# A conditioning projection with the raw fp32 weights as the stationary operand, and grouped softmax in two attentions

## The reference, cut to what matters

```python
# window attention, per head (width 64), keys of this block of 128 and the one before
sc = einsum('qd,kd->qk', q, k) * 64 ** -0.5            # masked
m = maximum(max(sc), sink); e = exp(sc - m)
o = (e / (sum(e) + exp(sink - m))) @ v
# latent attention, per head (96 score dimensions, 64 value dimensions), causal
o = softmax(einsum('qd,kd->qk', q, k) * 96 ** -0.5) @ v
# conditioning, for each of the second block's two layers
mod  = silu(c)     @ w_ada[layer] + b_ada[layer]       # [1024] @ [1024, 6144]
modc = silu(c_ctx) @ w_ada[layer] + b_ada[layer]
```

## Time and profile before

| | |
|---|---|
| median of 3 runs (lowest, highest) | 4760.0 us (4756.5, 4763.3) |
| the profiled execution, its time | 4758.1 us |
| its span, first to last instruction | 4756.3 us |
| mean granted TensorE clock | 0.862 |
| PE, PEld, DVE, ACT busy | 3654.1, 2957.5, 2821.0, 2143.9 us |
| DMA, mean over the span | 135 GB/s |

### The profile page before, as it was taken

The page is one execution under the profiler, slowest core; times in us unless marked ns, Lnnn a source line. Parts: engine busy times, 40 slices in busy tenths (PEclk is TensorE's granted clock), DMA queues, the critical chain, the costliest instruction groups (busy, mean ns, idle before and its releaser), DMA issues. The chain is left out here.

```text
span 4756.3 us, 53669 instructions
## 1 busy us (share of the span) xinstructions
PE 3654.1 (77%) x17794; PEld 2957.5 (62%) x17794; DVE 2821.0 (59%) x3774; ACT 2143.9 (45%) x2746; POOL 647.1 (14%) x256
## 2 busy tenths in 40 slices
PE   6975999836866999666975567699897957656987
PEld 5654777635755777445965356588776846345865
DVE  4654999955746999776444544444344555444545
ACT  3433999823526999644433202233232434113433
POOL 0003433400004344300000230000000000310000
PEclk9576999977877999888998777899998978768998
DMA  2014999921017999775211001111121220011222
GB/s 91 1 45 179 419 418 416 402 74 38 1 64 308 417 417 417 298 255 186 60 38 24 1 1 45 37 62 62 58 62 37 73 43 1 1 38 65 97 78 81
DMA packets 158177, 643.31 MB, mean 135 GB/s; under 512 B 43482, under 2 KB 55228, under 8 KB 94396
## 3 DMA queue, kind: packets, MB, share of 16 engines
q1 hardware_dynamic: 135116, 617.42, 34.4%
q0 software_dynamic: 10592, 16.81, 1.0%
q10 hardware_dynamic: 12312, 7.10, 0.7%
HBM read 636.82 MB, written 24.35 MB: 139 GB/s over the span
## 5 line engine op out<-in xcount | busy, mean ns | idle before, releaser
L1413 DVE TENSOR_TENSOR w_low<-w_raw,w_high 128x2048 fp32r<-128x2048 f32 x392 | 881.9, 2283 | 61.6 <-ACT w_high L1477 59.8
L1477 ACT CAST w_high<-w_raw 128x2048 fp32r<-128x2048 f32 x392 | 746.3, 1911 | 78.3 <-DMA w_raw<-in_moe_down_dram 39.2
L485 PE MATMUL banks<-w_high,x_high 128*128 128x512 f32 (+3 forms) x1324 | 518.7, 392 | 145.9 <-DVE w_low L437 134.1
L485 PE MATMUL banks<-w_low,x_high 128*128 128x512 f32 (+3 forms) x1324 | 505.3, 382 | 0.0
L404 ACT CAST w_high<-w_raw 128x512 fp32r<-128x512 f32 (+3 forms) x321 | 190.7, 594 | 695.2 <-PE banks L485 621.1
L485 PE MATMUL banks<-w_high,x_low 128*128 128x512 f32 (+3 forms) x1324 | 503.9, 381 | 0.0
L1317 PE MATMUL banks<-w_high,x_split 128*128 128x512 f32 x1024 | 417.7, 408 | 60.4 <-DVE w_low L1413 54.7
L1317 PE MATMUL banks<-w_low,x_split 128*128 128x512 f32 x1024 | 402.7, 393 | 0.0
L485 PEld LDWEIGHTS banks<-w_high,x_high 128*128 128x128 f32 x1324 | 256.5, 194 | 221.6 <-DVE w_low L437 165.8
L2380 PE MATMUL banks<-x_high,w_high 128*128 128x512 f32 (+1 forms) x1056 | 319.9, 357 | 38.5 <-DVE w_low L2420 38.5
L2380 PE MATMUL banks<-x_high,w_low 128*128 128x512 f32 (+1 forms) x1056 | 323.0, 360 | 0.0
(11 more groups left out here) (375 smaller groups left out, 6999.0 us busy)
## 6 DMA issues: line engine op xcount, KB each, us to landing
w_raw<-in_moe_gate_dram SPq DMA_DIRECT2D x132, 1024.0 KB
w_raw<-in_moe_up_dram SPq DMA_DIRECT2D x132, 1024.0 KB, 10.2
w_raw<-in_moe_down_dram SPq DMA_DIRECT2D x132, 1024.0 KB, 10.9
w_raw<-in_w_ada_dram SPq DMA_DIRECT2D x48, 1024.0 KB, 7.3
w_raw<-in_ffn_w_up_dram SPq DMA_DIRECT2D x44, 1024.0 KB
w_raw<-in_ffn_w_down_dram SPq DMA_DIRECT2D x88, 256.0 KB, 2.7
w_raw<-in_w_cols_dram SPq DMA_DIRECT2D x48, 256.0 KB, 2.6
y<-expert_rows SPq DMA_DIRECT2D x8, 1024.0 KB, 9.8
```

Of the source, the lines that this page charges most:

```text
L485: ins_ = pe.matmul(psum_of(g), st[:, rest % S, a:b], mv[:, rest % S, x:y], start=start and first + second == 0, stop=stop and first == 1)
L1413: dve.tensor_tensor(WS[1][:, v % LOW, :], WR[:, v % RAW, :], WS[0][:, v % HIGH, :].bitcast(F32), ALU.subtract).then_inc(low, 1)
L1477: act.copy(WS[0][:, v % HIGH, :], WR[:, v % RAW, :]).then_inc(high, 1)
```

## The change

`window_layer` and `latent_layer` call `grouped_attention` in groups of four heads. For the window layer a new `split_rows` casts and subtracts Q and K into fp32r halves: Q as [high, low] of a head side by side, K's high half twice and K's low half twice, so that after the transposes (24 groups of four, in place of 8 and 4) scores are two fp32r passes over 128 rows. `modulation` is rewritten: the raw weight tiles are the stationary operand, the two vectors two moving columns, and the results of both layers, already in column form, gather in one bank. The bias comes in column form from the host.

```diff
-                self.transpose("a_qT", groups)
...
-                self.transpose("a_kT", [([K2[:, t, h].rearrange("p a d -> p (a d)") for t in range(NT)],
-                                         KT[:, h, :], None, None) for h in range(A_KV)])
...
-                self.attention("a_attn", units, DH)
+                QT = self.sbuf(ctx, "qT", [P, A_HEADS, T], F32R)
+                KT = self.sbuf(ctx, "kT", [P, 2, A_KV, T], F32R)
+                with ExitStack() as c2:
+                    QS = self.sbuf(c2, "q_stacked", [P, NT, A_HEADS, 2, DH], F32R)
+                    KS = self.sbuf(c2, "k_stacked", [P, NT, 2, A_KV, 2, DH], F32R)
+                    self.split_rows(QKV, QS, KS)
+                    of = lambda x: x.rearrange("p a d -> p (a d)").bitcast(F32)
+                    self.transpose("a_qkT", [([of(KS[:, t, w, h]) for t in range(NT)], KT[:, w, h, :], None, None)
+                                             for w in range(2) for h in range(A_KV)] +
+                                   [([of(QS[:, t, h]) for t in range(NT)], QT[:, h, :], DH ** -0.5, None)
+                                    for h in range(A_HEADS)])
...
+                        groups.append(([
+                            ([(QT[:, h, t * P:(t + 1) * P], [KT[:, w, kv, a * P:(t + 1) * P]]) for w in range(2)],
+                             [mask[:, 0:2 * P] if t else mask[:, P:2 * P]], values)
+                            for h in range(kv * per, (kv + 1) * per)], self.sinks[:, kv * per:(kv + 1) * per],
+                            O[:, t, kv * per * DH:(kv + 1) * per * DH].rearrange("p (i d) -> p i d", i=per)))
+                self.grouped_attention("a_attn", groups, DH, False, 2)
...
+    def split_rows(self, QKV, QS, KS):
...
+            def _(act):
+                for t in range(NT):
+                    for half in range(2):
+                        act.copy(KS[:, t, 0, :, half, :], k[:, t]).then_inc(k_high, 1)
+                for t in range(NT):
+                    act.copy(QS[:, t, :, 0, :], q[:, t]).then_inc(q_high, 1)
+            def _(dve):
...
+                        dve.tensor_tensor(KS[:, t, 1, :, half, :], k[:, t], KS[:, t, 0, :, half, :].bitcast(F32),
+                                          ALU.subtract)
...
+                    dve.tensor_tensor(QS[:, t, :, 1, :], q[:, t], QS[:, t, :, 0, :].bitcast(F32), ALU.subtract)
...
-                self.attention("b_attn", units, B_DQ)
...
+                            units.append(([(QT[:, h, t * P:(t + 1) * P], [KT[:, h, 0:(t + 1) * P]])],
+                                          [causal[:, (NT - 1 - t) * P:T]],
+                                          [KV[:, c, v:v + B_V] for c in range(t + 1)]))
...
+                self.grouped_attention("b_attn", groups, B_V, False, 2)
...
     def modulation(self):
...
-            self.split("mod_split", [(CP[:, :, :], CS[0][:, :, :], CS[1][:, :, :])])
+        NV, JK = 2, 6 * KD
+        BLOCKS, UNIT, R = DEPTH * NM // BANK, KD * BANK // 2, 6
...
+            CP = self.sbuf(ctx, "c_padded", [P, KD, NV])
...
+                def _(sp):
+                    for n in range(2 * BLOCKS):
+                        if n >= R:
+                            sp.wait_ge(used, n - R + 1)
+                        sp.dma_start(WR[:, n % R, :], ins["w_ada"][n // 2][:, n % 2 * UNIT:(n % 2 + 1) * UNIT]).then_inc(
+                            raw_in[n % R], 16)
...
+                def _(act):
+                    act.dma_start(CR[:, :, :], ins["c_columns"]).then_inc(c_in, 16)
+                    act.dma_start(BT[:, :, :], ins["b_adaT"]).then_inc(bias_in, 16)
...
+                    act.activation(CP[:, :, 0:2], CR[:, :, :], ACT.Silu).then_inc(ready, 1)
...
+                def _(pe):
+                    for n in range(2 * BLOCKS):
+                        pe.wait_ge(raw_in[n % R], 16 * (n // R + 1))
+                        for j in range(4):
+                            for k in range(KD // 2):
+                                at = k * BANK + j * P
+                                ins_ = pe.matmul(result(n // 2, j), WR[:, n % R, at:at + P],
+                                                 CP[:, n % 2 * (KD // 2) + k, :], start=(n % FIRST == 0 and j + k == 0),
+                                                 stop=(n % 2 == 1 and k == KD // 2 - 1), skip_group_check=True)
+                        ins_.then_inc(used, 1)
...
+                        pe.transpose(self.ps[0:2 * JK, 6 + layer, 0:P], self.MC[:, layer, :],
+                                     self.const("ident")).then_inc(turned, 1)
...
+                def _(dve):
...
+                    dve.wait_ge(used, 2 * BLOCKS)
...
+                            dve.tensor_tensor(to, results(layer, v), bias, ALU.add).then_inc(added, 1)
...
+                        dve.tensor_copy(rows[:, layer, :], self.ps[0:2 * JK, 6 + layer, 0:P]).then_inc(out, 1)
...
-            self.load("mod_out", [(self.mod[layer], rows[:, layer, :]) for layer in range(DEPTH)])
-            self.load("mod_in", [(back[:, layer, :], self.mod[layer].rearrange("v (j p) -> (v j) p", p=P))
-                                 for layer in range(DEPTH)])
-            self.transpose("mod_T", [([back[:, layer, :]], self.MC[:, layer, :], None, None)
-                                     for layer in range(DEPTH)])
```

More of the change, by code:

```diff
@@ L949, in window_layer @@
                     self.rope_halves("a_rope", jobs)
[L951 to L955, removed]
-                self.transpose("a_qT", groups)
-                sem = self.Sems(self, "a_k2")
@@ L958, in window_layer @@
[L958 to L967, removed]
@@ L972, in window_layer @@
+                groups = []
+                per = A_HEADS // A_KV
                 for t in range(NT):
-                    for h in range(A_HEADS):
-                        r = (h % 2) * DH
+                    for kv in range(A_KV):
                         a = max(t - 1, 0)
                         mask = self.const("window")
[L977 to L984, removed]
@@ L1689, in modulation @@
         NM = 6 * DM
+        NV, JK = 2, 6 * KD
+        BLOCKS, UNIT, R = DEPTH * NM // BANK, KD * BANK // 2, 6
+        PER = BLOCKS // 6
+        FIRST = 2 * (PER if NV > 2 else BLOCKS)
         with ExitStack() as ctx:
+            sem = self.Sems(self, "mod")
+            raw_in = [sem(f"raw_in{u}") for u in range(R)]
+            c_in, bias_in, cleared, ready, used, added, turned, out, stored = (sem(n) for n in (
+                "c_in", "bias_in", "cleared", "ready", "used", "added", "turned", "out", "stored"))
@@ L1691, in modulation @@
             CR = self.sbuf(ctx, "c_columns", [P, KD, 2])
-            CP = self.sbuf(ctx, "c_padded", [P, KD, P])
-            CS = [self.sbuf(ctx, n, [P, KD, P], F32R) for n in ("c_high", "c_low")]
-            rows = self.sbuf(ctx, "mod_rows", [2, DEPTH, NM])
-            back = self.sbuf(ctx, "mod_tiles", [2 * 6 * KD, DEPTH, P])
-            self.load("mod_c", [(CR[:, :, :], ins["c_columns"])] +
-                      [(rows[:, layer, :], ins["b_ada"][layer:layer + 1, :].broadcast_to([2, NM]))
-                       for layer in range(DEPTH)])
@@ L1779, in modulation @@
-            self.end(sem)
-            self.load("mod_out", [(self.mod[layer], rows[:, layer, :]) for layer in range(DEPTH)])
-            self.load("mod_in", [(back[:, layer, :], self.mod[layer].rearrange("v (j p) -> (v j) p", p=P))
-                                 for layer in range(DEPTH)])
-            self.transpose("mod_T", [([back[:, layer, :]], self.MC[:, layer, :], None, None)
-                                     for layer in range(DEPTH)])
+                    dve.wait_ge(bias_in, 16)
```

131 lines of the change are left out of this document (57 added, 74 removed).

## The result

The changed kernel takes 4809.7 us (median of 4 runs, 4805.6 to 4816.0) against 4758.3 (4 runs, 4756.5 to 4763.3) for the kernel before on the same chip: ratio 1.0107, 95% interval 1.009 to 1.0125. It is slower, as forecast, but by 51 us and not by 88, and it lies 2.3 us under the forecast's range. The profiled execution took 4813.0 us (span 4811.2), 3.3 above the median.

What follows compares the result with a forecast made beforehand. Serial stages on one core, PE busiest at 77%, limits differing by stage. 4758 + 163 (modulation) - 62 (window attention with preparation) - 13 (latent attention) = 4846, with 1.9 added 4848 us; range 4812 to 4888.

Steps and rivals of the forecast that it cites:

- Modulation, the price of a pair: New modulation: each of 1536 weight-load/matmul pairs costs 0.217 us at clock 0.50, 333 us; whole stage +163 us.
- Modulation, its ends: Modulation before and after the pairs: PE starts near 2046, and 6 us follow its last pair.
- Window attention: Clock mostly rises, DVE leads at 1.15 us a unit: -75 us; with preparation -62 (bounds -36 and -69).
- The preparation: Window layer before its attention: casts, subtractions and 96 transposes instead of 48 add 13 us.
- four resources alike: Old modulation: DVE's subtraction, ACT's cast, PE and weight loads are near each other, none alone the bound.
- Latent attention: Grouping wins 0.1 to 0.3 us a unit by number of keys: -13 us (bounds 0 and -20).
- PE's work is unchanged: Latent attention: the change leaves PE's work as it was; no size given.
- short stretches at 1.00 in the modulation: Range's lower end, 4812: such stretches take back an eighth of the modulation's excess.
- 1: Modulation: the clock rises, a pair costs 0.116 us, stage 8 us longer than before, total 4693; chance 0.08.
- 2: Modulation: the weight load's pace does not hang on the clock, 0.117 us at 0.50, total 4695; chance 0.03.
- 3: Attentions stay at 0.50 and grouping wins little, -36 and -2 us, total 4885; chance 0.20.
- 4: Modulation: a matmul on a raw weight tile becomes three pairs, adding 167 us, total 5015; chance 0.02.

Runs made afterwards that it cites:

- run 5: Changed kernel with 128 moving columns (126 zero) in the modulation instead of 2, results added block by block: 4663.5 us, ratio 0.9814.
- run 6: Changed kernel with modulation weight tiles of 64 stationary columns instead of 128, twice as many load/matmul pairs: 4823.0 us in one run.
- run 8: Changed kernel with grouped window attention scored by one raw fp32 matmul on 64 rows, with the old preparation: 4877.5 us, ratio 1.0265.
- run 1: Changed kernel with the old modulation put back, so grouped attentions alone: 4661.0 us, ratio 0.9801.
- run 2: Kernel before the change with only the new modulation, attentions old: 4910.8 us, ratio 1.0324.
- run 3: Changed kernel with 32 moving columns (30 zero) in the modulation instead of 2: 4810.5 us, ratio 1.0117.
- run 4: Changed kernel with 64 moving columns (62 zero) in the modulation instead of 2, results added block by block: 4812.7 us, ratio 1.0119.
- run 10: Changed kernel with 64 moving columns in the modulation, all filled with the two vectors' values repeated: 4816.8 us, ratio 1.0137.
- run 9: Changed kernel with 30 unread raw fp32 matmuls of 512 moving columns ahead of the modulation's pairs: 4828.9 us, ratio 1.0162.
- run 12: Changed kernel with window scores as one raw fp32 matmul over 128 rows, Q twice against K over zeros: 4804.1 us, ratio 1.0099.

## Why the prediction was right in its sign and missed its range

- **Modulation, the price of a pair: right.** 0.217 was taken from the router, 0.2134 measured; 327.8 us for 333. The clock at 0.50, the full PE, the empty DVE and ACT and DMA near 150 GB/s came as forecast. The Trainium skill, page "TensorE: Matmul & The Clock Gate", section "LDWEIGHTS (loading the stationary operand)", has columns divided by 1.2 in nanoseconds and names no clock: 107 for 128 and 53 for 64. The traces do not agree for raw fp32 at 0.50, 213 and 107. At 1.00, with 128 moving columns, 111 is near it (run 5).
- **Modulation, its ends: near.** The start was put 5.8 us behind the first issue and took 7.0, since the vectors' load and the Silu's table were not covered by anything; the tail was put at 6 and took 4.2. With the pair's price this term came out 5.7 us too high.
- **Window attention: the clock right, the pace in part by luck, 8 us too small.** The clock rises, and a unit takes 1.13 us for 1.15. But DVE was to set this pace with 1.15 a unit, and its busy time from 150 to 206 is 42.03 us, or 0.85 a unit. PE has 0.97 a unit, near the 0.98 forecast, and waits for DVE's copies for the rest (the second line below). I kept 8 units of 256 keys at 0.50, 1.8 us each: the clock was up before the first of them (0.99 from 150), 5 us. The preparation took 10.1 us and not 13. The -70.4 lies just outside my bound of -69 because that bound took the attention's good end, 72 us, which held (74.4), and left the preparation at its central +13.
- **A row misread, without effect on the sum.** The 79.9 us of the earlier trace rows in which PE waited for DVE in the old modulation are mostly one wait of 71.3 from before the stream (the first line below). In the stream PE waited for DVE for 8.6 us and was busy for 139.64 of 152.70, so it was PE that was nearest to being the old stage's bound, and not four resources alike.

Waits: us in total, times, the longest. The first is of the kernel before, 2040 to 2222, the second of after, 150 to 204:

```profile
PE banks L1775 <- DVE w_low L1753: 79.9, 24, 71.3
```

```profile
PE banks L701 <- DVE expsT L764: 7.9, 13, 1.0
```

- **Latent attention: the step that failed.** -13 with bounds 0 and -20, measured -26.1. The step priced the 256 keys by ten microseconds at 1.00, 1225 to 1235, and gave the 128 and 384 keys 0.2 us a unit for which no row is named. The same rows gave 0.88 as the stage's mean clock, and a mean between two levels says that some stretch ran at 0.50; no term of the sum had that stretch. The runs show it as the 27.3 us from 1195.0 to 1222.3, in the units of 128 and the first units of 256 keys, and these two sizes won 17.2 us where 8.0 were forecast: 9 of the 13 us that were missed. The other 4 lie in the 384 and 512 keys, at 1.00 before and after. There it was waits of the old loop, most likely: PE was idle for 9.4 of its last 87.3 us. That "PE's work is unchanged" held for the records and not for their time, 105.45 us against 89.05. I had named the clock as what decides the window attention and did not carry that thought to the stage beside it.
- **The sum.** Against the profiled execution, 4846 forecast and 4813.0 measured, 33 us: 13.1 latent, 8.4 window, 5.7 modulation, 3.0 in stages before the modulation and 2.9 behind it that the diff does not touch. The median lies 3.3 under the profiled run, and the 1.9 added for the median of before makes up the rest.
- **The range** missed by 2.3 us. Its lower end allowed 14 us for the attentions' good bounds and some 22 for short stretches at 1.00 in the modulation (an eighth of the excess is 19 to 20; its own working ends near 4814). These stretches did not come. In their place came 21.5 us from the attentions, 7.5 beyond their bounds, 5.7 from the modulation's ends and pace, 5.9 from untouched stages and 5.2 from the median. The latent term is the largest of these: with it at -13 the time would have been near 4823, inside the range.
- **The rivals.** 1 did not occur, and run 5 shows that it was priced rightly (0.1136 for 0.116, a stage 3 us longer for 8) and what it would have taken. 2 is excluded: 128 columns took 0.2134 us at 0.50 and not 0.117, and the price goes with the columns and with the clock (runs 5, 6). 3 did not occur; run 8, with raw scores on 64 rows, is the nearest to it, and there grouping at 0.50 wins 5 us where the rival had 49. 4 did not occur: 1536 pairs.

## What to carry to other kernels

Price a product with a narrow moving side by its weight loads, at the clock that such a product itself gets, and look for a stretch of the same trace that has both; taking elementwise work off DVE and ACT is worth next to nothing while a PE at the low clock is the bound (run 8), and becomes necessary once the clock rises and their old busy time is longer than PE's new one. When a stage's mean granted clock lies between the two levels, cut it finer before you price it: the part at the low level is where a denser or wider form of the same work wins most. Judge a change of several parts part by part on the chip, since a gain of 96 us was hidden here behind a loss of 154 (runs 1, 2).

## What the runs showed of the hardware that was not expected

- A PE that is busy all the time, with loads back to back for 328 us, stays at 0.50 with 2, 32 or 64 moving columns, zeros or real values, and runs at 1.00 with 128 (runs 3, 4, 5, 10). Useless columns made the stage 154 us faster.
- The clock falls back from 1.00 to 0.50 with no idle time at all (run 9, PE busy for 6.00 of 6 and 5.00 of 5 us around it).
- Raw fp32 weight loads take two cycles of the granted clock for each stationary column at 0.50: 0.2134 us for 128 and 0.1067 for 64. At 1.00 a pair with 128 takes 0.111 us (run 5, 1960 to 2000), near two cycles of 2.4 GHz a column (0.107); there the 128 moving columns may set the pace as well.
- Scores on 64 rows stayed at 0.50 through 148 us with PE full; the same products over 128 rows, half of them zeros in one operand, ran at 1.00 (runs 8, 12). That the zero rows cost PE nothing that shows, and that the pace of a unit more than doubled (2.62 to 1.22 us), was the largest surprise; how much of it is the entry stays open, as said at run 12.
